# Query ropes on GpSimd, ScalarE's copies between the exps, the MLP's input by token half, a norm's root in the last input panel, and w_o's last tile added later

## What is computed

```python
u = rmsnorm(h, norm_mix)
aq, ak, av, dq, dk, dv, dz, db, da = split(u @ w_in)
aq, ak = rope(aq), rope(ak)                    # 8 query heads, 2 key heads of 64
attn_out = sliding_window_sink_attention(aq, ak, av, sinks)   # blocks of 128 tokens, each sees itself and the one before
dn_out = gated_deltanet(dq, dk, dv, dz, ...)   # chunked scan, RMS norm, gate silu(z)
h = h + concat(attn_out, dn_out) @ w_o
m = rmsnorm(h, norm_mlp)
h = h + square(relu(m @ w_up)) @ w_down
```

## Time and profile before

| | |
|---|---|
| median of 3 runs | 2119.77 us (2119.6 to 2123.96) |
| the profiled execution | 2125.43 us, its span 2123.6 us |
| granted TensorE clock, mean | 0.979 |
| TensorE (PE) busy | 2031.4 us, 96% of the span |
| VectorE (DVE), ScalarE (ACT), GpSimd (POOL) busy | 995.7, 716.3, 373.0 us |

### The profile page before, as it was taken

One profiled execution on the slowest core, in us unless ns is written; L12 is line 12 of the kernel. 1 busy time (PEld: TensorE's weight loads), 2 busy tenths in 40 slices (PEclk: granted clock), 3 DMA queues, 4 the chain that ended last, 5 costly groups with the idle time before them and its releaser, 6 DMA issues.

```text
span 2123.6 us, 24771 instructions
## 1 busy us (share of the span) xinstructions
PE 2031.4 (96%) x9957; PEld 1664.2 (78%) x9957; DVE 995.7 (47%) x1670; ACT 716.3 (34%) x1344; POOL 373.0 (18%) x429
## 2 busy tenths in 40 slices
PE   7999899889999999999999999999999999899999
PEld 6777688777777888888888888777988898676677
DVE  4556635654444333333333335535634436566641
ACT  4656212254343221212112123344211125555521
POOL 4042113620030000000000002255061316100100
PEclk9999999999999999999999999998999999899999
DMA  4134332221011111111111112012310132411123
GB/s 145 40 104 125 95 92 80 75 77 40 21 37 43 50 50 50 40 50 50 50 50 47 44 50 70 29 40 72 111 40 21 50 110 79 161 45 30 40 80 99
DMA packets 191050, 137.09 MB, mean 65 GB/s; under 512 B 34952, under 2 KB 176520, under 8 KB 190424
## 3 DMA queue, kind: packets, MB, share of 16 engines
q1 hardware_dynamic: 190936, 135.51, 21.1%
HBM read 108.17 MB, written 27.31 MB: 64 GB/s over the span
## 4 chain that ended last, share of the span: by engine, by line
PE 84%; DVE 7%; ACT 4%; POOL 2%; issue 1%; DMA 1%; SPq 0%; DVEq 0%; POOLq 0%; ACTq 0%
PE ps L314 22%; PE ps L315 22%; PE ps L316 22%; PE ps L327 4%; PE ps L2736 3%; PE ps L526 2%; PE ps L1237 1%; DVE wlo L300 1%; PE ps L2637 1%; PE ps L2725 1%; PE ps L2726 1%; PE ps L2727 1%; PE ps L1221 1%; DVE gtmp L720 1%; ACT sc L1267 1%
## 5 line engine op out<-in xcount | busy, mean ns | idle before, releaser
L314 PE MATMUL ps<-xh,whi 128*128 128x512 f32 (+2 forms) x1728 | 695.5, 403 | 17.1 <-DVE wlo L300 9.2
L315 PE MATMUL ps<-xl,whi 128*128 128x512 f32 (+2 forms) x1728 | 674.7, 390 | 0.0
L316 PE MATMUL ps<-xh,wlo 128*128 128x512 f32 (+2 forms) x1728 | 671.0, 388 | 0.0
L314 PEld LDWEIGHTS ps<-xh,whi 128*128 128x128 f32 x1728 | 331.8, 192 | 91.7 <-issue 18.4
L316 PEld LDWEIGHTS ps<-xh,wlo 128*128 128x128 f32 x1728 | 331.5, 192 | 66.3
L315 PEld LDWEIGHTS ps<-xl,whi 128*128 128x128 f32 x1728 | 332.2, 192 | 61.3 <-issue 3.1
L294 ACT ACTIVATE whi<-wraw 128x1024 fp32r<-128x1024 f32 (+1 forms) x143 | 145.5, 1018 | 356.3 <-PE ps L316 341.3
L300 DVE TENSOR_TENSOR wlo<-wraw,whi 128x1024 fp32r<-128x1024 f32 (+1 forms) x143 | 187.6, 1312 | 123.3 <-ACT whi L294 123.2
L314 PE MATMUL ps<-ffh,whi 128*128 128x512 f32 x512 | 199.4, 389 | 0.0
L315 PE MATMUL ps<-ffl,whi 128*128 128x512 f32 x512 | 199.3, 389 | 0.0
L316 PE MATMUL ps<-ffh,wlo 128*128 128x512 f32 x512 | 199.2, 389 | 0.0
(11 more groups left out here) (435 smaller groups left out, 2549.6 us busy)
## 6 DMA issues: line engine op xcount, KB each, us to landing
wraw<-w_in SPq DMA_DIRECT2D x47, 512.0 KB, 3.9
wraw<-w_up SPq DMA_DIRECT2D x32, 512.0 KB, 4.0
wraw<-w_down SPq DMA_DIRECT2D x32, 512.0 KB, 3.5
xt<-x SPq DMA_DIRECT2D x8, 512.0 KB, 7.0
wraw<-w_o SPq DMA_DIRECT2D x8, 512.0 KB, 3.5
xr<-x SPq DMA_DIRECT2D x8, 512.0 KB, 3.7
wraw<-w_ple_gate SPq DMA_DIRECT2D x8, 512.0 KB, 4.2
h_d<-hT SPq DMA_DIRECT2D x8, 512.0 KB, 2.7
```

Of the source, the lines that this page charges most:

```text
L314: pe.matmul(out, h, xh[:, xk, c0:c1_], start=(n == 0), stop=False)
L315: pe.matmul(out, h, xl[:, xk, c0:c1_], start=False, stop=False)
L316: mm = pe.matmul(out, l, xh[:, xk, c0:c1_], start=False, stop=(n == nk - 1))
```

## The change

1. All eight query blocks are roped by GpSimd: blocks 4 to 7 in panels 18 to 21, blocks 0 to 3 in slots 6 and 7 of w_o. VectorE ropes none.
2. In panel 22 the attention steps of block 4 and the key transposes go ahead of the mixed step of their slot, and the norm's square root stands in its slot 7; "values" moves to slot 0.
3. In every slot of w_o ScalarE takes its steps in a new order (`copies_between`): norm, then part 3 (sink and three exps), then the copies, then parts 4 and 5.
4. The MLP's XH and XL are made for c0 = 512 first, from the moment that w_o's last tile of that half is done, then for c0 = 0. The last tile of w_o (7, 0) is added to hT by VectorE behind the fourth XL tile, and the squares of n = 7 stand behind the halves.
5. w_up's panel 0 goes through c0 = 512 first. Panel 2's weights are split ahead of panel 0's read-outs, on VectorE between the two reciprocals.

```diff
 (project_dve)
-                    w.wait_ge(*dve_in.at("rope", NB - 2))
...
-            if 18 <= i < 22:
-                for b in (2 * (i - 18),):
...
-                    rope(dve, w, tq[:, b, :]..., rt, dve_in, ("rope", b))
+    def query_rope_pool(pool, w, b):
+        first = {0: 7}.get(b, b - 1 if b != 4 else None)
+        w.wait_ge(*act_in.at("turned", "aq", 3, 1))
...
+        if first is not None:
+            w.wait_ge(*pool_in.at("q rope", first))
+        if b < 4:
+            w.wait_ge(*pe_in.at("turn", "av", 0, 1))
+        rope(pool, w, tq[:, b, :]..., rt[2:4], pool_in, ("q rope", b))
 (project_pool)
-                b = 2 * (i - 18) + 1
...
+                query_rope_pool(pool, w, 4 + i - 18)
     def last_panel_steps():
-        out = [[("mixed", k, 0)] for k in range(4, 8)]
-        out[0].append(("keys", 0, 0))
-        for t, steps_ in enumerate(lane_steps(0)[0:3]):
-            out[1 + t] += steps_
-        return out
+        out = [[("keys", 0, 0)]] + lane_steps(0)[0:3]
+        out[3] = out[3] + [("norm", 1, 0)]
+        return [steps_ + [("mixed", 4 + t, 0)] for t, steps_ in enumerate(out)]
     def mixer_plan():
-        slots[0].append(("norm", 1, 0))
-        slots[1] += [("norm", 1, 1), ("values", 0, 0)]
+        slots[0].append(("values", 0, 0))
+        slots[1].append(("norm", 1, 1))
...
+            slots[6 + b // 2].append(("rope", b, 0))
+    def copies_between(slot):
+        place = {3: 0, 4: 2, 5: 2}
+        return sorted(slot, key=lambda step: 0 if step[0] == "norm" else place.get(step[2], 1) if step[0] == "attend" else 1)
 (mix_pe)
-                w.wait_ge(*(pool_in.at("q rope", i) if i % 2 else dve_in.at("rope", i)))
+                w.wait_ge(*pool_in.at("q rope", i))
 (wo_act)
-                for step in slot:
+                for step in copies_between(slot):
...
+            if n < 7:
+                wo_square(act, w, n, c0)
 (wo_dve)
+            if (n, c0) != (7, 0):
+                joined(dve, w, "wo", n, c0, dve_wo.at("ev", "wd", n, c0))
+    def up_cols(g, f):
+        return HALVES[::-1] if g == f == 0 else HALVES
 (up_act; up_dve likewise)
-            act_split(act, w, up_panel(g, f) + 1)
+            if (g, f) != (0, 1):
+                act_split(act, w, up_panel(g, f) + 1)
             if g == f == 0:
                 stats_act(act, w, pe_ml, act_ml, ("stats", "mlp"))
+                act_split(act, w, up_panel(0, 1) + 1)
 (up_dve)
+                stats_dve(dve, w, act_ml, dve_ml, ("stats", "mlp"), (512,))
+                dve_split(dve, w, up_panel(0, 1) + 1)
+                stats_dve(dve, w, act_ml, dve_ml, ("stats", "mlp"), (0,))
     def mlp_act(act, w):
-        w.wait_ge(*pe_wo.end())
-        normed_act(act, w, V("g_mlp"), range(8), ...)
+        for half in (512, 0):
+            w.wait_ge(*pe_wo.at("wo", 7, half))
+            normed_act(act, w, V("g_mlp"), range(8), ..., halves=(half,))
+            wo_square(act, w, 7, half)
     def mlp_dve(dve, w):
-        w.wait_ge(*pe_wo.end())
-        normed_dve(dve, w, V("g_mlp"), range(8), ...)
+        for half in (512, 0):
+            w.wait_ge(*pe_wo.at("wo", 7, half))
+            for ks in (range(4), range(4, 8)):
+                normed_dve(dve, w, V("g_mlp"), ks, ..., halves=(half,))
+                if half and ks[0] == 0:
+                    joined(dve, w, "wo", 7, 0, dve_wo.at("ev", "wd", 7, 0))
```

More of the change, by code:

```diff
@@ L399, in stats_act, with stats_dve @@
             act.activation(RST[:, c0:c0 + 512], tile(*key, c0), ACT.Sqrt, scale=1.0 / T, bias=eps[:, 0:1]).then_inc(*done.up("sqrt", *key, c0))
-    def stats_dve(dve, w, act_done, done, key):
-        for c0 in (0, 512):
+    def stats_dve(dve, w, act_done, done, key, halves=(0, 512)):
+        for c0 in halves:
             w.wait_ge(*act_done.at("sqrt", *key, c0))
@@ L987, in rope @@
         eng.tensor_tensor(b, b, t[1], ALU.add).then_inc(*done.up(*key))
+    def query_rope_pool(pool, w, b):
+        first = {0: 7}.get(b, b - 1 if b != 4 else None)
+        w.wait_ge(*act_in.at("turned", "aq", 3, 1))
+        w.wait_ge(*pool_in.at("conv", "v", 3))
+        w.wait_ge(*dve_in.at("conv", "v", 3, 2))
+        w.wait_ge(*ld_c1.at())
+        if first is not None:
+            w.wait_ge(*pool_in.at("q rope", first))
+        if b < 4:
+            w.wait_ge(*pe_in.at("turn", "av", 0, 1))
+        rope(pool, w, tq[:, b, :].rearrange("p (h d) -> p h d", h=8), 8, 32, cosv[:, b, :], sinv[:, b, :], rt[2:4], pool_in, ("q rope", b))
     def project_pool(pool, w):
@@ L1380, in mix_pool @@
     def mix_pool(pool, w, kind, k, hf):
+        if kind == "rope":
+            query_rope_pool(pool, w, k)
         if kind == "mixed" and k >= 4:
@@ L1445, in wo_act, with wo_square, joined @@
                 act_split(act, w, WO0 + n // 2 + 1)
-            i = 2 * n + c0 // 512
-            w.wait_ge(*dve_wo.at("ev", "wo", n, c0))
-            if i >= 4:
-                w.wait_ge(*pool_wo.at("sum", i - 4))
-            act.activation(sqn[i % 4][:], hT[:, n, c0:c0 + 512], ACT.Square).then_inc(*act_wo.up("square", i))
-    def wo_dve(dve, w):
-        def added(name, n, c0, ready):
-            d = hT[:, n, c0:c0 + 512]
-            w.wait_ge(*pe_wo.at(name, n, c0))
-            w.wait_ge(*ready)
-            dve.tensor_tensor(d, d, tile(name, n, c0), ALU.add).then_inc(*dve_wo.up("ev", name, n, c0))
+            if n < 7:
+                wo_square(act, w, n, c0)
+    def wo_square(act, w, n, c0):
+        i = 2 * n + c0 // 512
+        w.wait_ge(*dve_wo.at("ev", "wo", n, c0))
+        if i >= 4:
+            w.wait_ge(*pool_wo.at("sum", i - 4))
+        act.activation(sqn[i % 4][:], hT[:, n, c0:c0 + 512], ACT.Square).then_inc(*act_wo.up("square", i))
+    def joined(dve, w, name, n, c0, ready):
+        d = hT[:, n, c0:c0 + 512]
+        w.wait_ge(*pe_wo.at(name, n, c0))
+        w.wait_ge(*ready)
+        dve.tensor_tensor(d, d, tile(name, n, c0), ALU.add).then_inc(*dve_wo.up("ev", name, n, c0))
+    def wo_dve(dve, w):
         for t, (n, c0) in enumerate(wd_tiles):
@@ L1464, in wo_dve @@
                     mix_dve(dve, w, *step)
-            added("wd", n, c0, act_wo.at("res", n, 1))
+            joined(dve, w, "wd", n, c0, act_wo.at("res", n, 1))
         for t, (n, c0) in enumerate(wo_tiles):
@@ L1468, in wo_dve @@
                 dve_split(dve, w, WO0 + n // 2 + 1)
-            added("wo", n, c0, dve_wo.at("ev", "wd", n, c0))
+            if (n, c0) != (7, 0):
+                joined(dve, w, "wo", n, c0, dve_wo.at("ev", "wd", n, c0))
             if t == 0:
@@ L1593, in mlp_act @@
     def mlp_act(act, w):
-        w.wait_ge(*pe_wo.end())
-        normed_act(act, w, V("g_mlp"), range(8), lambda k, c0: dve_wo.at("ev", "wo", k, c0), act_ml)
+        for half in (512, 0):
+            w.wait_ge(*pe_wo.at("wo", 7, half))
+            normed_act(act, w, V("g_mlp"), range(8), lambda k, c0: dve_wo.at("ev", "wo", k, c0), act_ml, halves=(half,))
+            wo_square(act, w, 7, half)
         up_act(act, w, 0)
@@ L1611, in mlp_dve @@
     def mlp_dve(dve, w):
-        w.wait_ge(*pe_wo.end())
-        normed_dve(dve, w, V("g_mlp"), range(8), lambda k, c0: dve_wo.at("ev", "wo", k, c0), act_ml, dve_ml)
+        for half in (512, 0):
+            w.wait_ge(*pe_wo.at("wo", 7, half))
+            for ks in (range(4), range(4, 8)):
+                normed_dve(dve, w, V("g_mlp"), ks, lambda k, c0: dve_wo.at("ev", "wo", k, c0), act_ml, dve_ml, halves=(half,))
+                if half and ks[0] == 0:
+                    joined(dve, w, "wo", 7, 0, dve_wo.at("ev", "wd", 7, 0))
         up_dve(dve, w, 0)
```

16 lines of the change are left out of this document (5 added, 11 removed).

## The result

The changed kernel takes 2103.51 us (median of 4, 2100.46 to 2105.12) against 2119.68 us (2117.17 to 2123.96) for the kernel before, run beside it. The ratio is 0.9914, with a 95% interval of 0.9901 to 0.9926: between 15.7 and 21.0 us. The forecast was 2099.0 us in a range of 2092 to 2109; it was 4.5 us too fast. The profiled execution of the changed kernel took 2105.12 us; its span is 2103.3 us, 20.3 us less than before, where the forecast had 23.1.

A forecast was written before the change was run, and what follows sets the result against it. TensorE, busy 96% of the span, was taken as the bound, so time comes from its gaps and lower-clock stretches. 10.6 + 0.4 + 2.1 + 10.0 = 23.1 us; 2119.77 - 23.1 + 2.3 = 2099 us, range 2092 to 2109.

The forecast's parts named there:

- Part 1: Query ropes to GpSimd: Xs waits in panels 18 to 22 go, 7.7 us, clock falls 3.2, key ropes -0.3: 10.6 us gained.
- the key ropes: Panel 22: TensorE comes earlier to key transposes that wait for GpSimd's last key rope: -0.3 us, ends 0 and -3.
- The four late ropes: Slots 6 and 7 of w_o: 24 added GpSimd instructions of about 0.9 us cost nothing; bounds 0 and -1.8 us.
- the slower-than-before rival: Slots 6 and 7: GpSimd's late ropes set the end; slower from 4.1 us per instruction, 2145 us at 5; chance 0.03.
- Part 2: Panel 22, slots 0 and 1: ScalarE work leaves tav's way, later work nearly cancels it: +0.4 us, ends -1 and +3.1.
- Part 3: ScalarE's order in w_o slots: qTb waits 3.5 us less, clock +1.4, late copies -2.8: +2.1 us, from -4 to +5.
- The late copy: Slots 3, 11, 19, 27: the probabilities' copy stands behind exps: -1.9 us in slot 11, -2.8 in all.
- The clock: Behind the first of the last three qTb waits, scores and dense tile avoid half speed: +1.4 us, or 0.
- the copies become the bound: Rival: all four late copies in w_o cost 1.9 us and a clock fall of 1.6 each: 2110 us; chance 0.15.
- Part 4: MLP entry: no wait between w_o and w_up, 7.8 us, and panel 2's weight split in time, 2.2: 10.0 us.
- The race at equal pace: MLP entry: VectorE's XL tiles and TensorE's slices both take 0.70 us; some 0.7 us head start left, no wait.
- The other rivals: New wait replaces the ropes, 2104 us, chance 0.10; MLP race lost, 2105, 0.07; change does nothing, 0.02.

The follow-up runs named there:

- p3_order: Kernel before the change with only ScalarE's new order in the w_o slots (`copies_between`): 2124.18 us against 2120.45, ratio 1.0019.
- p4_mlp: Kernel before the change with only the new MLP entry (XL and XH by token half, panel 2's weights split early): 2112.76 us, ratio 0.9957.
- p2_panel: Kernel before the change with only the new order of panel 22 and slots 0 and 1: 2121.35 us against 2120.45, ratio 1.0.
- after: The changed kernel with the whole change, against the kernel before it: 2103.51 us against 2119.68, ratio 0.9914.
- p1_ropes: Kernel before the change with only the query ropes moved to GpSimd: 2107.76 us against 2122.74, ratio 0.9938.
- a_old_order: Changed kernel with ScalarE's old order inside the w_o slots put back: 2100.07 us, ratio 0.9904 to the kernel before.
- a_both: Changed kernel with the probabilities' copy ahead of the sink and first three exps, and the last two sums of squares on VectorE: 2094.27 us, ratio 0.9876.
- a_sums_dve: Changed kernel with the last tile's two sums of squares on VectorE behind its XL tiles, instead of GpSimd: 2102.0 us, ratio 0.9905.
- a_copy_first: Changed kernel with the copy of the other block's probabilities ahead of the sink and first three exps: 2095.89 us, ratio 0.9877.
- b_no2: a_both with panel 22 and slots 0 and 1 back in the order before the change: 2096.85 us, ratio 0.987.
- b_qfirst: a_both with the copy qTb ahead of all exps in every slot: 2095.11 us, ratio 0.9869.
- b_slot0: a_both with qTb and tav copied ahead of all exps in slot 0 alone: 2095.78 us, ratio 0.9879.

## Why the prediction was right, and where it was not

**Part 1, forecast 10.6 us, measured 10.3.** The Xs waits went (7.7), the two falls of the clock behind them too, and the key ropes cost 0.7 to 1.1 us instead of 0.3, inside the bounds. With part 1 alone it is 10.6. That this is the forecast to a tenth is luck: 10.6 - 7.7 + 0.7 leaves 3.6 us for the two falls where 3.2 was forecast, and the two misses cancel. So is the number of falls, which the forecast took from one profile: p3_order and p4_mlp show two for the same three waits, behind the first and the third, and p2_panel three, with an A to B that is 2.7 us longer. The four late ropes cost nothing, as forecast: GpSimd's timeline in after, first and last of the 24:

```profile
461.48 0.75 POOL L971 TENSOR_TENSOR rt<-tq,c 128x256 f32<-128x256 f32 x1
...
478.61 0.73 POOL L978 TENSOR_TENSOR tq<-tq,rt 128x256 f32<-128x256 f32 x1
```

They end at 479.3, and are 0.72 to 0.75 us each, not 0.9; the slower-than-before rival needed 4.1. Nor did they hold up VectorE in a way that reaches TensorE: B to C is 130.54 us in p1_ropes and 130.52 before.

**Part 2, forecast +0.4, measured -0.4 to -0.9 alone.** The step held that the copies trade places and little is won; the sign was wrong, inside its bounds (-1 to +3.1). The copies did trade places, with 0.3 us won at the scores; what the step left out of the sum is the new wait of 0.9 us for the read-out of the values, and the residual's copies cost 0.4 more. What it did not see either is that part 2 and part 3 act together: part 2 puts qTb behind all eight exps (a wait of 3.9 us in p2_panel and a_old_order), and part 3 takes five of them from its way (2.4).

**Part 3, forecast +2.1, measured -1.05 alone by the ruler and -4 by the ratio (-1.3 to -6.6).** This is the step that failed, and of its three terms it was one, the clock. The qTb waits: forecast 3.5 us less, measured 4.2 - 0.7 = 3.5 in p3_order and 4.2 - (3.6 - 2.4) = 3.0 in after. The late copy: forecast 2.8, measured 2.2 and 2.5, with 1.8 in slot 12 where 1.9 was forecast. The clock: forecast +1.4, and that was half of the account. (The row behind it was read too strongly: the scores at 485.28 took 1.33 us, 1.14 where the clock holds, so the lower clock began within them; the granted 0.66 from 485 to 490 us shows the fall.) The fall behind slot 8's wait does go: from the product before it to the one behind it took 495.20 - 476.23 = 19.0 us before and 477.99 - 461.22 = 16.8 in a_both, 2.2 less, of which 1.98 - 0.95 is the wait and 1.2 the clock. But a new one comes behind a value product that waits. The stretches between value products tell its price. From slot 4's product to the next it took 467.65 - 449.39 = 18.3 us in after and 461.22 - 445.73 = 15.5 in a_both, 2.8 more; from slot 12's to the next 497.67 - 482.88 = 14.8 in a_sums_dve, 507.47 - 492.69 = 14.8 in p3_order and 489.48 - 477.99 = 11.5 in a_both, 3.3 more. All three kernels with part 3 as it stands have one such fall behind slot 4's or slot 12's product; all five with the old order (before, p1_ropes, p2_panel, p4_mlp, a_old_order) have theirs behind slot 8's wait; and none of the five with the copy ahead of the exps (a_copy_first, a_both, b_no2, b_qfirst, b_slot0) has any between 450 and 575 us. The two parts of the clock term together are +1.2 - 3.3 = -2.1 us in p3_order where +1.4 was forecast, and 3.5 - 2.2 - 2.1 = -0.8 is close to the -1.05 of the ruler. The forecast charged a fall only in the rival "the copies become the bound" (1.6 for each of four); the truth lies between: two of the four copies are late, and one of them brings a fall, at twice the price that I took from the earlier trace rows. Part of that rival is what happened: it cost 2.5 + 2.8 us in after, where the rival had 7.6 + 6.4.

**Part 4, forecast 10.0, measured 8.5 in after.** TensorE runs from w_o into w_up without a wait, and panel 2's split is in time (2.2 forecast; from the statistics to panel 2's first matmul it is 654.16 - 638.94 = 15.22 before and 635.22 - 622.27 = 12.95 after, so 2.27). The race at equal pace was won, as argued. In a_sums_dve, a_both and three more C to D is 62.65 to 62.67 us, 70.69 - 62.65 = 8.0 less than before, where 7.8 was forecast. What failed is one sentence, "the last tile's squares are summed by about a microsecond before the statistics need them". They were late by 1.58. VectorE's timeline in after, and GpSimd's:

```profile
610.84 8.03 DVE L1525 SCALAR_TENSOR_TENSOR xl<-hT,vec,xh 128x512 fp32r<-128x512 f32 x12
618.79 2.31 DVE L300 TENSOR_TENSOR wlo<-wraw,whi 128x1024 fp32r<-128x1024 f32 x1
```

```profile
605.47 1.29 POOL L1498 TENSOR_TENSOR accn<-accn,sqn 128x512 f32<-128x512 f32 x1 [0.55 <-ACT sqn L1458]
612.44 9.78 POOL L1498 TENSOR_TENSOR accn<-accn,sqn 128x512 f32<-128x512 f32 x2 [5.68 <-ACT sqn L1458]
```

The two sums take 9.78 us, not 2 x 1.29. The first starts 1.60 us into VectorE's twelve XL tiles and ends at 620.0, 1.1 us behind the last of them (610.84 + 8.03 = 618.87), so it seems to have done its own 1.29 us of work only when VectorE had passed. The second takes 2.2 us, beside a weight split of VectorE that takes 2.31 us instead of 1.22. That moving the sums to VectorE takes 1.76 us off shows the cost; the cause, who holds what, is read below.

**The total.** Forecast against measured, profiled execution against profiled execution: part 1 10.6 and 10.3, parts 2 and 3 together +2.5 and -0.3, part 4 10.0 and 8.5; 23.1 and 18.5. The other 1.8 us of the 20.3 lie before A and behind panel 2, where nothing was changed. Of the 4.6 us that are missing, 2.8 are parts 2 and 3 and 1.5 part 4, where GpSimd's late sum cost 1.76; no rival named it. So the likeliest case held for parts 1 and 4 and not for part 3, where the copies, the rival named first, did part of their harm. By the medians the forecast was 20.8 us (23.1 less 2.3 for clock falls in the surplus of one execution) and 16.2 were measured; no run tests the 2.3. (The range was said to take in the first rival, but it ended at 2109 and that rival stood at 2110.) The other rivals did not occur: the key ropes bound panel 22 by 0.7 to 1.1 us and not by half of part 1, and w_up's first tile has no wait in after.

## To carry to other kernels

Price a late instruction by its wait and by what the clock may do behind it: here one late copy of 0.7 us was followed by a fall that cost 2.8 more, and one of 1.8 us by none, so a new wait that the forecast already sees should carry a clock term too, with a range, as the removed ones did. When an order is changed to bring one copy forward, list what it pushes back in the slots where the first copy does not occur: here the same sort key shortened waits in slots 8, 16 and 24 and made copies late in slots 3 and 11, and one more key, the copy ahead of the exps, turned a loss of 1 us (131.57 against 130.66, B to C) into a gain of 4 (126.60), each from one profile. And if an engine's queue has no gap, moving one of its instructions may only move the wait; compare fixed marks in the traces, not medians, to see gains under 2 us.

## What was unexpected of the hardware

**A run of two-input instructions of VectorE can keep GpSimd out for most of its length.** Every XL tile reads hT and XH from SBUF, and the sum reads two tiles too. In after all sixteen XL tiles take 739 to 752 ns and the sum 7575 ns; it waited through nine of them. In a_copy_first, with the same two programs and the sum again starting 1.60 us into the twelve tiles (603.91 - 602.31), it went the other way. The same tile and engine rows there, XL on VectorE and the sum on GpSimd:

```profile
L1525 DVE SCALAR_TENSOR_TENSOR xl<-hT,vec,xh x16: 737/743/1790, 599.1 to 611.7; 128x512 fp32r<-128x512 f32 x16
```

```profile
L1498 POOL TENSOR_TENSOR accn<-accn,sqn x2: 1625/1744/1862, 603.9 to 609.3; 128x512 f32<-128x512 f32 x2
```

The sums take 1.6 and 1.9 us, the twelve tiles 10.12 us instead of 8.03, two of them 1.79 and 1.78 instead of 0.74, one beside each sum, and TensorE waits 0.8 us for XL instead of 1.58 for the sum. p4_mlp and a_old_order look like a_copy_first. So of four profiles with this arrangement GpSimd got in at once in three and was kept out in one, and either way it costs: C to D is 1.3 us longer than without the sums in the one case, 1.76 in the other. What decides it lies below what the trace resolves. The Trainium skill (SBUF — State Buffer, "two separate sides") says that the shared pair of ports is an exclusive lock, which the one that starts first holds for its whole instruction while the other fully blocks. The two stretched tiles, each 1.05 us longer, agree. That the loser waits until the first instruction finishes does not cover the 7.58 us: nine instructions of the winner went by. The prediction used this rule for the ropes in the slots, where all 24 instructions took 0.72 to 0.75 us, and not for the entry of the MLP, where the change itself put GpSimd's sums beside sixteen such tiles.

**The clock falls behind small waits.** In after a wait of 0.73 us (behind another of 0.61) is followed by some ten microseconds of which most are at the lower clock, and the 1.82 us wait in slot 12 by none; in p3_order and a_sums_dve it is the 1.82 us that brings the fall and the 0.33 and 0.34 us waits that don't. Here windows of 5 us in after (window, length, busy and count of PE, PEld, DVE, ACT and POOL, granted clock, DMA share, GB/s):

```profile
450.00:455.00 5.00, 5.00 (x32) 4.81 (x32) 0.90 (x4) 3.79 (x12) 2.50 (x2) 0.71 0.02 3
455.00:460.00 5.00, 4.89 (x23) 4.11 (x23) 1.52 (x3) 1.47 (x3) 0.98 (x1) 0.61 0.00 0
460.00:465.00 5.00, 4.65 (x34) 3.52 (x32) 2.02 (x5) 2.10 (x5) 4.84 (x7) 1.00 0.35 105
```

The length of the wait does not decide it. In eleven of the thirteen profiles the clock also falls at the first scores of block 5 or just behind them, between 430 and 455 us. After and a_copy_first have no fall there, behind the same wait of 2.39 us that brings one in a_sums_dve and a_both. And a_sums_dve has a fall behind a wait of 0.85 us (granted 0.53 from 519 to 521) that every other kernel with part 3 has without one. So how many falls a kernel has is partly chance from one execution to the next. Which wait brings a fall was not tested by itself and stays open; what the runs show is that the falls behind Xs, behind slot 8's wait and behind the value products are gone in every profile in which those waits are gone, or halved in slot 8.
